# From the w_o projection to the first up tiles: GpSimd's adds taken out, w_o evacuated and scaled on ScalarE, two feature tiles per VectorE operation, the first up weights split ahead

## The reference, cut to what matters

```
mix = (sigmoid(g_a) * (A @ w_attn_out) + sigmoid(g_b) * (R @ w_ret_out)) @ w_o
x   = x + RMSNorm_post(mix)                       # gain norm_mix_post
h   = RMSNorm_pre(x)                              # gain norm_ffn_pre
x   = x + RMSNorm_post(relu(h @ w_up)^2 @ w_down)
```

## Time and profile before

| | us |
|---|---|
| three executions | 899.95, 900.01, 902.49 (median 900.01) |
| the profiled execution: its time | 901.57 |
| the profiled execution: span from first to last instruction | 899.7 |
| TensorE busy with matmuls | 876.5 (97%) |
| VectorE busy | 468.2 (52%) |
| ScalarE busy | 302.2 (34%) |
| GpSimd busy | 57.9 (6%) |

### The profile page before, as it was taken

One profiled execution on the slowest core, in us unless ns is written; L12 is line 12 of the kernel. 1 busy time (PEld: TensorE's weight loads), 2 busy tenths in 40 slices (PEclk: granted clock), 3 DMA queues, 4 the chain that ended last, 5 costly groups with the idle time before them and its releaser, 6 DMA issues.

```text
span 899.7 us, 16798 instructions
## 1 busy us (share of the span) xinstructions
PE 876.5 (97%) x6908; PEld 858.3 (95%) x6908; DVE 468.2 (52%) x741; ACT 302.2 (34%) x444; POOL 57.9 (6%) x49
## 2 busy tenths in 40 slices
PE   6999999999999999999996999999999999999997
PEld 6999999999999999999995899999999999999995
DVE  6323667666786677666338543334433443334336
ACT  5211546444531111454324332123312331133322
POOL 1000000000000000000435200000000000000223
PEclk9999999999999999999996999999999999999997
DMA  9222212321312131122221122222222222232202
GB/s 299 92 94 93 85 47 83 105 71 58 120 63 85 53 101 54 48 94 94 94 93 48 48 92 70 75 93 93 94 94 93 92 68 75 91 95 93 94 1 100
DMA packets 78456, 77.28 MB, mean 86 GB/s; under 512 B 2944, under 2 KB 76304, under 8 KB 78416
## 3 DMA queue, kind: packets, MB, share of 16 engines
q1 hardware_dynamic: 69328, 70.53, 24.3%
q10 hardware_dynamic: 8448, 4.02, 1.6%
q0 software_dynamic: 640, 2.17, 0.7%
HBM read 71.70 MB, written 4.99 MB: 85 GB/s over the span
## 4 chain that ended last, share of the span: by engine, by line
PE 94%; DVE 3%; issue 1%; DMA 1%; ACT 1%; SPq 0%; ACTq 0%; DVEq 0%
PE acc L749 78%; PE wk L749 3%; PE wk L773 3%; PE wk L887 3%; DVE scaled L1414 1%; DVE act_lo L1434 1%; PE wk L849 1%; PE wk L848 1%; DMA x_nat<-in_x_prompt 1%; PE wk L956 1%; PE wk L806 1%; PE wk L965 1%; PE wk L797 1%; PE wk L954 0%; PE wk L840 0%
## 5 line engine op out<-in xcount | busy, mean ns | idle before, releaser
L471 ACT ACTIVATE w_hi<-w_raw 128x1024 fp32r<-128x1024 f32 x123 | 130.4, 1060 | 475.8 <-PE acc L749 460.5
L749 PE MATMUL acc<-act_hi,w_hi 128*128 128x272 f32 x1264 | 268.3, 294 | 9.3 <-DVE act_lo L1434 8.6
L749 PE MATMUL acc<-act_hi,w_lo 128*128 128x272 f32 x1264 | 263.9, 290 | 0.0
L749 PE MATMUL acc<-act_lo,w_hi 128*128 128x272 f32 x1264 | 263.1, 290 | 0.0
L749 PEld LDWEIGHTS acc<-act_hi,w_hi 128*128 128x128 f32 x1264 | 200.5, 190 | 14.4 <-DVE act_lo L1434 9.8
L749 PEld LDWEIGHTS acc<-act_lo,w_hi 128*128 128x128 f32 x1264 | 200.9, 191 | 0.0
L749 PEld LDWEIGHTS acc<-act_hi,w_lo 128*128 128x128 f32 x1264 | 199.8, 191 | 0.0
L1113 DVE TENSOR_TENSOR w_lo<-w_raw,w_hi 128x1024 fp32r<-128x1024 f32 x123 | 150.5, 1224 | 36.5 <-ACT w_hi L471 36.3
L749 PE MATMUL acc<-mid_hi,w_hi 128*128 128x272 f32 x608 | 125.4, 287 | 0.0
L749 PE MATMUL acc<-mid_hi,w_lo 128*128 128x272 f32 x608 | 125.0, 288 | 0.0
L749 PE MATMUL acc<-mid_lo,w_hi 128*128 128x272 f32 x608 | 124.8, 287 | 0.0
(11 more groups left out here) (195 smaller groups left out, 778.2 us busy)
## 6 DMA issues: line engine op xcount, KB each, us to landing
w_raw<-in_w_in SPq DMA_DIRECT2D x44, 512.0 KB, 4.4
w_raw<-in_w_ff_up SPq DMA_DIRECT2D x32, 512.0 KB, 4.4
w_raw<-in_w_ff_down SPq DMA_DIRECT2D x32, 512.0 KB, 4.2
w_raw<-in_w_o SPq DMA_DIRECT2D x8, 512.0 KB, 4.3
x_nat<-in_x_prompt SPq DMA_DIRECT2D x4, 512.0 KB, 5.2
w_raw<-in_w_attn_out SPq DMA_DIRECT2D x4, 512.0 KB, 3.5
w_raw<-in_w_ret_out SPq DMA_DIRECT2D x4, 512.0 KB, 4.5
k_cache<-in_cache_attn_k SPq DMA_DIRECT2D x1, 1024.0 KB, 11.7
```

The source lines that it names most:

```text
L471: act.activation(w_hi[:, v % 2], w_raw[:, v // 2, :, P * (v % 2):P * (v % 2) + P], ACT.Copy).then_inc(hi_ready, 1)
L749: ins = pe.matmul(dst[:, n, 0:HALF], w[:, k, :], h[:, k, HALF * n:HALF * n + HALF], start=begin, stop=end)
```

## The change

ScalarE takes over the evacuation of w_o: it squares each tile straight from PSUM and writes y_mix already multiplied by the gain norm_mix_post, before it splits the next weights. VectorE adds the squares (`mix_add`). For the residual VectorE takes two feature tiles per operation: one product with wk, read twice by a broadcast, and one sum into xT; ScalarE squares two tiles at once, and VectorE adds these squares after the last act_lo. GpSimd keeps the clearing of y_ffn and its work in the last norms. All four tiles of the first up group have weight sets and accumulators of their own: TensorE takes three of them step by step and the fourth afterwards, with the second norm's sums and `spread` in the middle of the fourth, written to free columns of acc and wk. In all norms after the first the sums of both sources accumulate in PSUM, and ScalarE takes the root of the sums directly, with scale 1/1024 and epsilon as bias. The diff, cut to its core (removed functions stand in the listing above):

```diff
+        W_SETS = ((w_hi_third[:], w_lo_third[:]), (w_hi_fourth[:], w_lo_fourth[:]), (w_hi[:, 0], w_lo[:, 0]), (w_hi[:, 1], w_lo[:, 1]))
...
+        UP_DST = (acc[0], acc[1], wk_halves[1], wk_halves[0])
+        FINAL_SUM = wk[:, SUM_COL:SUM_COL + 5]
...
+        X1_RSTD = [acc[0][:, 0, 320:448], acc[0][:, 1, 320:448], acc[1][:, 0, 320:448], acc[1][:, 1, 320:448], wk_halves[1][:, 0, 320:320 + DEC]]
+        X1_SUM = acc[0][:, 0, 304:309]
...
-            order.after(pool.memset(sqsum[:], 0.0))
-            for m in range(KT):
-                if m % 2:
-                    pool.wait_ge(scaled_ready, m // 2 + 1)
-                    pool.tensor_tensor(xT[:, m, :], xT[:, m, :], scaled[:, m % 4, :], ALU.add).then_inc(x1_odd, 1)
-                if m > 1:
-                    add_square(2, m - 2)
-            add_square(2, KT - 2)
...
+            def root(norm, sums, tiles=range(5)):
+                act.wait_ge(sum_mm, norm)
+                prompt = slice(tiles[0], min(tiles[-1] + 1, 4))
+                ins = act.activation(tok_rstd[:, prompt], sums[:, prompt], ACT.Sqrt, scale=1.0 / D, bias=eps[:, 0:1])
+                if tiles[-1] == 4:
+                    ins = act.activation(tok_rstd[0:DEC, 4:5], sums[0:DEC, 4:5], ACT.Sqrt, scale=1.0 / D, bias=eps[0:DEC, 0:1])
+                ins.then_inc(std_ready, 1)
...
+            def mix_out(m):
+                if m >= 2:
+                    act.wait_ge(mix_added, max(1, m - 2))
+                act.activation(halves(sq[:, m % 2, :]), acc[m % 2][:, :, 0:HALF], ACT.Square).then_inc(mix_sq, 1)
+                act.activation(halves(y_mix[:, m, :]), acc[m % 2][:, :, 0:HALF], ACT.Copy, scale=gains[:, 1, m:m + 1]).then_inc(mix_y, 1)
+                act.activation(W_SETS[j][0], w_raw[:, v // 2, :, P * (v % 2):P * (v % 2) + P], ACT.Copy).then_inc(hi_ready, 1)
+            def x1_pair(p):
+                act.wait_ge(x1_ready, p + 1)
+                for m in (2 * p, 2 * p + 1):
+                    act.activation(act_hi[:, m, :], xT[:, m, :], ACT.Copy, scale=gains[:, 2, m:m + 1]).then_inc(h2_hi, 1)
+                if p == 3:
+                    act.wait_ge(x1_added, 1)
+                to = (x1_sums, sq, relu, sq)[p]
+                act.activation(to[:], xT[:, 2 * p:2 * p + 2, :], ACT.Square).then_inc(x1_sq, 1)
             for m in range(KT):
+                act.wait_ge(mm_done, 4 * G_WO + m + 1)
+                mix_out(m)
+                if m < 6:
+                    split_ahead(G_WO + m // 4, m % 4)
+                if m == 5:
+                    split_set(0, 0, 32 * (G_FFN + 1))
+                if m == 6:
+                    split_set(1, 1)
+                    split_set(2, 2, 32 * (G_FFN + 1))
+            root(1, FINAL_SUM)
+            x1_pair(0)
+            split_set(3, 3)
+            for p in range(1, 4):
+                x1_pair(p)
+            split_ahead(G_FFN, 2)
+            root(2, X1_SUM)
...
+                    if first and j == 0:
+                        split_ahead(g, 3)
...
+            def token_sums(out, sources, tiles=range(5)):
+                for t in tiles:
+                    s, n = TILES[t]
+                    for i, src in enumerate(sources):
+                        ins = pe.matmul(out[0:n, t:t + 1], src[:, s:s + n], ones[:, 0:1], start=(i == 0), stop=(i == len(sources) - 1))
...
-            feature_sum(1, squares_added(1, KT - 1), KT)
+            pe.wait_ge(mix_added, KT - 2)
+            pe.wait_ge(mix_sq, KT)
+            token_sums(FINAL_SUM, (sqsum, sq[:, 1, :]))
             spread(1)
...
+            def up_step(j, k):
+                if k == 0:
+                    pe.wait_ge(lo_ready, 4 * G_FFN + j + 1)
+                ins = products(UP_DST[j], *W_SETS[j], k, act_hi, act_lo, k == 0, k == KT - 1)
+                if k == KT - 1:
+                    ins.then_inc(mm_done, 1)
             for k in range(KT):
                 pe.wait_ge(h2_lo, k + 1)
-            feature_sum(2, squares_added(2, KT - 1), 2 * KT)
+                for j in range(3):
+                    up_step(j, k)
             for k in range(KT):
-            column_tile(G_FFN, 3, act_hi, act_lo)
+                if k == 2:
+                    pe.wait_ge(x1_added, 3)
+                    token_sums(X1_SUM, (x1_sums[:, 0, :], x1_sums[:, 1, :]))
+                if k == 5:
+                    spread(2, places=X1_RSTD)
+                up_step(3, k)
...
+            def final_sums(part):
+                pe.wait_ge(sq_added, squares_added(KT - 1 + part))
+                pe.wait_ge(sq_ready, KT + 2 * part)
+                token_sums(FINAL_SUM, (sqsum, sq[:, 1, :]), PART_TILES[part])
...
-                dve.wait_ge(sum_mm, n)
-                order.after(dve.tensor_scalar(tok_last[:, cols], wk[:, a + 5:b + 5], 1.0 / D, EPS, ALU.mult, ALU.add))
-                dve.scalar_tensor_tensor(tok_var[:, cols], wk[:, a:b], 1.0 / D, tok_last[:, cols], ALU.mult, ALU.add).then_inc(var_ready, 1)
+            def norm_rstd(n, tiles=range(5)):
...
+            def mix_add(m):
+                dve.wait_ge(mix_sq, m + 1)
+                if m > 1:
+                    dve.wait_ge(mix_added, m - 1)
+                dve.tensor_tensor(sqsum[:], sq[:, 0, :] if m == 1 else sqsum[:], sq[:, m % 2, :], ALU.add).then_inc(mix_added, 1)
+            for m in range(6):
+                if m:
+                    mix_add(m)
+                split_ahead(G_WO + m // 4, m % 4)
+            split_set(0, 4 * G_FFN, 0)
+            mix_add(6)
+            split_set(1, 4 * G_FFN + 1, 1)
+            split_set(2, 4 * G_FFN + 2, 2)
...
+            def x1_pair(p):
+                b = 2 * (p % 2)
+                if p >= 2:
+                    dve.wait_ge(x1_ready, p - 1)
+                order.after(dve.tensor_tensor(scaled[:, b:b + 2, :], y_mix[:, 2 * p:2 * p + 2, :],
+                                              wk[:, 0:T].unsqueeze(1).to_broadcast([P, 2, T]), ALU.mult))
+                dve.tensor_tensor(xT[:, 2 * p:2 * p + 2, :], xT[:, 2 * p:2 * p + 2, :], scaled[:, b:b + 2, :], ALU.add).then_inc(x1_ready, 1)
+            def x1_add(p):
+                dve.wait_ge(x1_sq, p + 1)
+                if p > 1:
+                    dve.wait_ge(x1_added, p - 1)
+                dve.tensor_tensor(x1_sums[:], x1_sums[:], (None, sq, relu, sq)[p][:], ALU.add).then_inc(x1_added, 1)
+            norm(1, range(5))
+            dve.wait_ge(mix_y, KT)
+            x1_pair(0)
             h2_low(0)
+            x1_pair(1)
+            h2_low(1, 2)
+            x1_pair(2)
+            h2_low(3, 4)
+            x1_pair(3)
+            h2_low(5, 6, 7)
+            split_set(3, 4 * G_FFN + 3, 3)
+            for p in range(1, 4):
+                x1_add(p)
+            norm_rstd(2)
+            dve.wait_ge(spread_mm, 3)
+            dve.tensor_copy(rstd[:, 0:256].rearrange("p (n c) -> p n c", n=2), acc[0][:, :, 320:448])
+            dve.tensor_copy(rstd[:, 256:512].rearrange("p (n c) -> p n c", n=2), acc[1][:, :, 320:448])
+            order.after(dve.tensor_copy(rstd[:, 512:T], X1_RSTD[4]))
...
-                    src = wk_halves[1] if first and j == 2 else acc[j % 2]
+                    src = UP_DST[j] if first else acc[j % 2]
...
                     evacuate(0)
+                    split_ahead(g, 2)
                     evacuate(1)
                     hidden_low(0)
                     hidden_low(1)
-                for j in range(2 if first else 0, 4):
+                    evacuate(2)
+                    split_ahead(g, 3)
+                    evacuate(3)
+                    hidden_low(2)
+                    hidden_low(3)
```

More of the change, by code:

```diff
@@ L152, in build @@
         tok_rstd = place("tok_rstd", [P, 8])
[L153 removed]
+        eps = place("eps_sb", [P, 8])
         rope = place("rope_sb", [P, 2, T])
@@ L681, in up @@
                     g = G_FFN + 4 * c + i
-                    if not (first and j < 2):
+                    if not first:
                         split_ahead(g, j)
@@ L785, in _, with spread @@
                 ins.then_inc(x_tr, 1)
-            def feature_sum(norm, added, squares, tiles=range(5)):
-                for col, src in ((SUM_COL, sqsum[:]), (SUM_COL + 5, sq[:, 1, :])):
-                    if col == SUM_COL:
-                        pe.wait_ge(sq_added, added)
-                    else:
-                        pe.wait_ge(sq_ready, squares)
-                    for t in tiles:
-                        s, n = TILES[t]
-                        ins = pe.matmul(wk[0:n, col + t:col + t + 1], src[:, s:s + n], ones[:, 0:1], start=True, stop=True)
+            def token_sums(out, sources, tiles=range(5)):
[3 more added lines that the diff above has]
+                        ins = pe.matmul(out[0:n, t:t + 1], src[:, s:s + n], ones[:, 0:1], start=(i == 0), stop=(i == len(sources) - 1))
                 ins.then_inc(sum_mm, 1)
-            def spread(norm, tiles=range(5), at=0):
+            def spread(norm, tiles=range(5), at=0, places=None):
                 pe.wait_ge(tok_rstd_ready, norm + 1)
```

(21 more changed lines are left out.)

122 lines of the change are left out of this document (43 added, 79 removed).

## The result

The changed kernel takes 894.91 us (median of five executions, 894.34 to 896.00) where the kernel before, run beside it, takes 900.92 (899.95 to 902.49): a ratio of 0.9933, 95% interval 0.9918 to 0.9948. It is faster, as forecast, by 6.0 us of the 7.7 that I had expected. The result lies inside the stated range, which reached to 895.8. The profiled execution of the changed kernel took 894.39 us, span 892.6.

What follows compares the result with a forecast made beforehand. Bound between w_o and the second up group by TensorE's waits for late act_lo, slowed beside GpSimd's adds, and a low clock. 8.3 us won, 0.6 lost in the last norm: 7.7, so 892.3 us on the median, range 890 to 895.8.

Steps and rivals of the forecast that it cites:

- w_o at no cost: w_o evacuation: a 3.7 us chain on ScalarE and VectorE is covered by 6.02 per tile; extra cost zero.
- First act_lo: First low part of the residual, ahead of the first up product: at 483.05 us, 0.2 earlier than before.
- Pairs: Residual on VectorE: paired product and sum 1.29 us each, each later pair 4.15 us with low parts and waits.
- The dearer broadcast (2.4): Residual product with wk read twice: at the most 2.4 us, against the 1.29 taken.
- the first rival: VectorE still sets the pace in the residual: 3.5 to 6 us won, 894 to 896.5; chance 0.18.
- The pace of three tiles per step: First up group: 2.26 us per step, TensorE slower than VectorE; 13 slow matmuls, then act_lo always ahead.
- The new wait: Behind the fourth up tile, TensorE waits for the next group's first low part, from 511.95 to 512.6.
- One rise of the clock and no fall until the end: Sign of being right, first up group: clock rises once near 486.1, then no gap lets it fall.
- Last norm, plus 0.6: Last norm: six more instructions ahead of the transposes and last spread cost 0.6 us, between 0 and 0.8.
- the rival that the change doesn't reach its target: VectorE's long operations not due to GpSimd: act_lo stays near 1.57, win 0 to 2.5 us, 897.5 to 900; chance 0.06.

Runs made afterwards that it cites:

- the twelve adds: Changed kernel with twelve GpSimd additions of zeros into the cleared y_ffn put back beside VectorE's residual; 899.53 us, ratio 0.9978.
- two tiles per step: Changed kernel with only the first two up tiles taken step by step, the third in a loop of its own; 896.76 us, ratio 0.9955.
- the run of all three: Changed kernel with second norm's sums spread out, first feature tile alone, last norm's sums as before, and spread at k = 4; 892.62 us, ratio 0.9910.

## Why the prediction was right, and which term was too large

- **w_o at no cost: right.** From 423 to 471 us TensorE is busy for all 48.00 us. The chain is 0.63 (square) + 0.71 (copy) + 1.06 + 1.22 = 3.6 us against 3.7 forecast and 6.02 per tile.
- **First act_lo: right.** The first up product comes 11.07 us behind w_o's last products, before 11.35: 0.28 sooner, forecast 0.2. The roots with a pointer for epsilon took 0.26 and 0.24, together 0.40 to their end, as taken.
- **Pairs: right.** 1.28 and 1.29 against 1.29; a pair every 4.13 us against 4.15 (the sum there had each low part at 0.74 and waits beside it; it was 0.78 and no waits). The dearer broadcast (2.4), on which the first rival rested, was not found.
- **The pace of three tiles per step: right, with luck in the clock.** It rose 3.0 us behind the first product, as forecast, but in the second profile of the same code 3.5 and in the others up to 6.1, so 13 slow matmuls were the low end of 13 to 27. Eight steps took about 19.6 us (21.09 less the first 12 matmuls of the fourth tile) against 19.4, and act_lo was never late.
- **The new wait: right in kind.** The three copies of rstd took 0.42, 0.41 and 0.18, the evacuation 0.72, the split 1.22; forecast 0.95, 0.72, 1.22. The wait was 0.39 against 0.65, as the tile's other half took 2.52 us behind `spread` and not 2.25.
- **"One rise of the clock and no fall until the end": wrong**, and this is the term that was mis-sized. The fourth tile was put at 6.02 + 2.1 + 1.3; its 18 matmuls behind the sums took 3.88 in place of 2.26. I had taken the clock of 1.00 behind the same sums in the earlier trace rows as a property of the sums, and it was one outcome. With the 1.6 us the stage would have won 8.4 against 8.3 forecast; spread-out sums give it back.
- **Last norm, plus 0.6: the order costs 0.3 to 0.5, and no loss of time is shown.** `spread` came 1.24 us later against its square (3.16 against 1.92), the rest of it the clock. From the square to the end it was 0.44 longer in the two profiles, but eight profiles with that tail lie between 14.7 and 16.4 us and three with the older one at 15.3 to 15.6.
- The rival that VectorE still sets the pace shows what it would have been when the third tile is taken out of the step (2.5 us of the stretch, 1.4 against the profile with an equally late clock); the rival that the change doesn't reach its target shows in the twelve adds (3.9 and 2.9 us). The two overlap, in the waits and in the clock, so they are not shares that add up to the stage's 6.77.
- The forecast of 892.3 stood on a median of 900.01; over five executions that median is 900.92. 0.9 of the 2.6 us between forecast and result are this, 1.6 the fall.
- That the time came out inside the range is in part luck. The forecast as worked out ended at 894; the 894.91 us lies in the part that was added for the first rival, and that rival's waits did not occur. What brought the time there, the fall of the clock behind the sums, was in neither, nor was the median of the kernel before, 0.9 us higher than taken.

The version to keep is the changed kernel with the sums spread out: faster than the kernel before by 0.9% in both series, and below the changed kernel's interval in the first (0.9907 [0.9892, 0.9923] against 0.9940 [0.9924, 0.9956]).

## What to carry to other kernels

Where a VectorE operation takes twice its time elsewhere in the same trace, look at what GpSimd does beside it before anything else, and count which operands come from SBUF. Give the engine that is fed so much work per step that it is slower than its feeder (here 4.5 us against 4.13 for two steps); pairing operations to save their fixed cost is worth nothing where the first one stands on the path and the others don't. Be wary of a block of tiny matmuls in one piece inside a dense stretch: here the clock fell behind 20 of them in seven of seven profiles of the new order, though not in the kernel before, and stayed up in three of three where they went a few at a time among full matmuls.

## What the runs showed that I had not expected

- The granted clock can fall while TensorE never waits: 5.87 us busy of 5.87, and 0.50 from 506 to 508, behind 2.06 us of one-column matmuls. The Trainium skill, "TensorE: Matmul & The Clock Gate", section "HAM oscillation — how this bites in real kernels", gives gaps in which TensorE is idle as the cause of such falls; here there was none, and the measurement decides.
- The time from the first up product to the rise of the clock varies: 3.0, 3.0, 3.4, 3.5, 3.9, 4.4, 5.0 and 6.1 us in eight profiles with three tiles per step and GpSimd quiet. At half speed that is up to 1.5 us, as much as the edits here were worth. Counted from the fall during the first norm it varies less: the low stretch lasted 10.2 us in six of the eight and 13.6 in two, those with 5.0 and 6.1, and 10.2 in the kernel before. (The runs with the twelve adds and with two tiles per step have 13.6 as well.) The rise did not follow an earlier first product: in the three runs that have one it came 12.6, 13.2 and 15.2 us behind the first sum, in the five others at 12.8 to 13.3 and once at 15.2. That hid the earlier start in the run of all three.
- The low clock near 16 us is there in one execution and not in another of the same code: in the two profiles of the changed kernel w_o's last products start at 470.95 and at 472.95 us. A difference of two single profiles must be cut at such places before a step is credited with it.
